# Attention in pairs: both branches of a head in one round of TensorE, values as two half-column products

## The chip, the cores and the metric

The kernel runs on one core of a Trainium2 chip. The metric is device time in microseconds of one execution. TensorE multiplies, ScalarE (ACT) and VectorE (DVE) move results out of PSUM and do the element-wise work, GpSimd (POOL) and SyncE (SP) start transfers. A profile of one execution gives start and duration of each instruction.

## The reference, cut to what matters

Two layers, each a token mixer and a mixture of experts, on 512 tokens of width 1024. The mixer has two attention branches with 8 heads each: A, sliding-window attention over at most two blocks of 128 keys with a bias and a sink, and B, latent attention over all blocks up to the present one. For both, per head:

```python
# A: s = q k^T * scale - slope * |distance|, sink joins the softmax
p = jnp.exp(s - m); p = p / (jnp.sum(p, axis=-1, keepdims=True) + jnp.exp(sink - m))
o = jnp.einsum('bcgrqk,bckgd->bcqgrd', p.astype(v.dtype), vb)      # head width 64
# B: s = (qn kn^T + qr kr^T) * scale, chunk-causal mask
p = jax.nn.softmax(s, axis=-1)
return jnp.einsum('bhqk,bkhd->bqhd', p.astype(v.dtype), v)         # head width 64
```

The outputs of both branches are projected, gated with sigmoid(h @ w_gate + b_gate) and added to x; then come routing and experts.

## The kernel before, in words

Each engine has one instruction stream, written out by hand; semaphores in a table S join them. The attention stage of a layer goes over 64 units u (NUN = 64): tile t = u // 16 of 128 queries, head h = (u // 2) % 8, branch b_ = u % 2 (0 is A, 1 is B). nk key blocks belong to a unit: t + 1 for B, at most 2 for A. For a unit the work is:

- TensorE, scores(u), L1822: scores into ps[u % 2], so all A units use ps[0] and all B units ps[1]. A unit waits until the maximum of the A unit before has been taken (negm_done), a B unit until the exponential of the B unit before is done (exp_done). In tile 0 the A product is 64 rows deep (L1835), in later tiles it is two fp32r products (L1839, L1840); B is one fp32 product, two records in the trace (L1844).
- VectorE, L1284 (A, a custom operation that writes sa and the maximum) or L1290 (B): the maximum.
- ScalarE, L847 (A, in place in sa, two buffers) or L853 (B, from ps[1] to pr): exponential and its sum; a second small instruction reads the accumulator and signals exp_done.
- TensorE, L1893: nk transposes of the probabilities into ps[3] (A) or ps[4] (B).
- ScalarE L861 copies ps[3] into ptr_a, VectorE L1300 copies ps[4] into ptr_b, one buffer each. Each waits for the values of the same branch's unit before: pv_done >= w - 1 for unit w.
- TensorE, L1909: values, nk products of 128x128 probabilities with 128x64 values into ps[2] or ps[6], four units side by side in a bank.
- VectorE, finish_pair (L1243, L1248): after four units it normalises them into `on`.

TensorE's loop, L1873: in step u it issues scores(u + 1), one gate chunk (six fp32r passes of 512 columns, L1663 to L1665, for u from 1 to 60), the transposes of u and the values of u - 1. At u % 16 = 3 and 6 of tiles 1 to 3 the finished outputs of the tile before are turned (out_turned, L1865) into banks 7 and 5.

Between these, ScalarE's and VectorE's loops over u carry work that TensorE needs later: on ScalarE the gate eviction (gate_out, L835, u % 4 = 1), the high part of the turned outputs (attn_out, L825, u % 16 = 4 and 7), quarters of a weight unit's high part (split_quarter, L655, u % 8 = 1 to 4) and the high part of queries (u = 10, 12, 21, 22, 37, 38); on VectorE the low part of the turned outputs (attn_low, L1090, u % 16 = 4 and 7, behind attn_out), halves of a weight unit's low part (split_half, L1058, u % 8 = 5 and 6), and the low part of queries (rows_low, L1090, u = 12, 15, 23, 24, 39, 40). VectorE's order in a step is: maximum of u; copy to ptr_b of u - 1 (u even); finish_pair (u % 4 = 2); attn_low; rows_low; split_half. ScalarE's is: exponential of u; copy to ptr_a of u - 1 (u odd); attn_out; gate_out; rows_high; split_quarter. The gate product's first chunk of a bank waits for attn_low of that bank.

Behind attention stand the output projections and the experts. There four experts share the array in column tiles of 32 (L2006, L2038), next to full-array products (L1997, L2018).

Of the kernel before, what the change touches and what calls it, by code (L numbers as in the profile page):

```python
# [23 lines left out]
P = 128  # L24
CHUNK = 64
A_KV, A_DIM = 2, 64
# [9 lines left out]
def hybrid_trunk(nc, x, positions, norm_mix, w_in, sinks, q_norm, w_qb, kv_norm, w_kvb, w_gate, b_gate,  # L36
# [3 lines left out]
    NT, KD = T // P, D // P  # L40
    AH = sinks.shape[1]
    AQ = AH * A_DIM
    QR, KVR = w_qb.shape[1], w_kvb.shape[1]
    HEADS = AH
# [4 lines left out]
    VD = w_kvb.shape[2] // HEADS - NOPE  # L49
# [54 lines left out]
    with ctx:  # L104
# [24 lines left out]
        ident = sb("ident", [P, P])  # L129
# [60 lines left out]
        av = sb("av", [P, NT, A_KV * A_DIM], F32, 42 * KB)  # L190
        v = sb("v", [P, NT, HEADS * VD], F32, 44 * KB)
# [14 lines left out]
        pr = sb("pr", [P, T], F32, 148.25 * KB)  # L206
        ptr_a = sb("ptr_a", [P, 2 * P], F32, 150.25 * KB)
        ptr_b = sb("ptr_b", [P, T], F32, 151.25 * KB)
        sa = sb("sa", [P, 2, 2 * P + 8], F32, 153.25 * KB)
# [80 lines left out]
        ps = [ctx.enter_context(nc.psum_tensor(f"ps{i}", [P, 512], F32)) for i in range(8)]  # L290
# [13 lines left out]
        S = {n: sem(n) for n in d_names}  # L304
# [1353 lines left out]
        def _(pe):  # L1658
            MM = nc.tensor.matmul
# [16 lines left out]
            for l in range(L):  # L1676
# [42 lines left out]
                for k in range(KD):  # L1719
# [9 lines left out]
                    for m in range(AH // 2 + 1):  # L1729
                        if (k, m) == (0, NT):  # L1730
                            pe.wait_ge(S["h1l_done"], NT + 1)
                        last = mm3(ps[m][:, :], *part(n, k, m * P, P), h1h[:, k, :], h1l[:, k, :], k == 0, k == KD - 1)
# [43 lines left out]
                for i in range(NT + 1):  # L1776
                    if i < NT:
                        o, tok = 4 * (i % 2), slice(i * P, (i + 1) * P)
# [5 lines left out]
                        for half in range(2):  # L1784
                            for k in range(KQ):
                                n = n0 if k < 2 else n0 + 1
                                last = mm3(ps[o + half][:, 0:hq], ch[:, k, tok], cl[:, k, tok],
                                           *part(n, k, half * hq, hq), k == 0, k == KQ - 1)
# [6 lines left out]
                        for two in range(2):  # L1795
                            for k in range(KKV):
                                wk = [w.rearrange("p (h two d) -> p two h d", two=2, d=NOPE)[:, two]
                                      for w in part(n0 + 2, k, 0, HEADS * 2 * NOPE)]
                                last = mm3(ps[o + 2 + two][:, :], ch[:, KQ + k, tok], cl[:, KQ + k, tok], *wk,
                                           k == 0, k == KKV - 1)  # L1800
                        last.then_inc(S["qkv_ps" if i < NT - 1 else "unit_used"], 1)
                    if i >= 1:
                        t, o = i - 1, 4 * ((i - 1) % 2)
                        pe.wait_ge(S["q_roped"], t + 1)
                        for h in range(HEADS):
                            last = nc.tensor.transpose(ps[o + h // 4][0:QD, (h % 4) * P:(h % 4 + 1) * P],
                                                       qc[t % 2][:, h, :], ident[:, :])
# [4 lines left out]
                        for h in range(HEADS):  # L1812
                            last = nc.tensor.transpose(ps[o + 2 + h // 4][0:QD, (h % 4) * P:(h % 4 + 1) * P],
                                                       kc[t % 2][:, h, :], ident[:, :])
# [3 lines left out]
                NUN = NT * 2 * HEADS  # L1818
# [3 lines left out]
                def scores(u):  # L1822
                    t, h, b_ = u // (2 * HEADS), (u // 2) % HEADS, u % 2
                    if u >= 2:
                        pe.wait_ge(S["exp_done" if b_ else "negm_done"], u - 1)
                    if u == 1:
                        pe.wait_ge(S["pool_in"], 32)
                    dst, tok = ps[u % 2], slice(t * P, (t + 1) * P)
                    if b_ == 0:
                        k0 = max(t - 1, 0) * P  # L1830
                        g = h // (AH // A_KV)
                        rows = slice(g * A_DIM, (g + 1) * A_DIM)
                        j, cols = h % (AH // A_KV), slice(k0, (t + 1) * P)
                        if t == 0:
                            last = MM(dst[:, 0:P], aq[rows, 0, j, :], ak[rows, cols], start=True, stop=True)  # L1835
                        else:
                            if h == 0:
                                pe.wait_ge(S["al_done"], 2 * A_KV + t * A_KV)
                            MM(dst[:, 0:2 * P], qs[t][:, g, j, :], ks[:, g, cols], start=True, stop=False)  # L1839
                            last = MM(dst[:, 0:2 * P], qs[t][:, g, j, :], kx[:, g, cols], start=False, stop=True)  # L1840
                    else:
                        n = (t + 1) * P
                        rows = slice(0, QD + NT)
                        last = MM(dst[:, 0:n], qt[rows, h, tok], kt[rows, h, 0:n], start=True, stop=True)  # L1844
                    last.then_inc(S["s_ps"], 1)

                def gate_chunk(m, i):
                    n = U_G[0] + m // 2
                    if i == 0:
                        weights_in(n)  # L1850
                        if m == 0:
                            pe.wait_ge(S["qt_ev"], 2 * NT)
                        if m >= 2:
                            pe.wait_ge(S["g_ev"], m - 1)
                        if m >= 4 and m % 4 == 1:
                            pe.wait_ge(S["otl_done"], 2 * (m // 4) - 1)
                        if m >= 4 and m % 4 == 2:
                            pe.wait_ge(S["otl_done"], 2 * (m // 4))
                    for k in (2 * i, 2 * i + 1):
                        a, c = part(n, k, (m % 2) * P, P)  # L1860
                        last = mm3(ps[7 if m % 2 else 5][:, :], a, c, h1h[:, k, :], h1l[:, k, :], k == 0, k == KD - 1)
                    if i == 3:
                        last.then_inc(S["unit_used" if m % 2 else "g_ps"], 1)

                def out_turned(t, br_, bank):  # L1865
                    pe.wait_ge(S["on_done"], 4 * t + 4)
                    for k in range(KO):
                        last = nc.tensor.transpose(ps[bank][:, k * P:(k + 1) * P], on[:, br_, k * P:(k + 1) * P],
                                                   ident[:, :])
                    last.then_inc(S["ot_ps"], 1)  # L1870

                scores(0)
                for u in range(NUN + 1):  # L1873
                    if u >= 2 * HEADS and u < NUN and u % (2 * HEADS) == 6:
                        pe.wait_ge(S["g_ev"], (u - 2) // 4)
                        out_turned(u // (2 * HEADS) - 1, 1, 5)
                    if u + 1 < NUN:
                        scores(u + 1)
                    if 1 <= u <= 4 * (2 * KD - 1):
                        gate_chunk((u - 1) // 4, (u - 1) % 4)  # L1880
                    if u >= 2 * HEADS and u < NUN and u % (2 * HEADS) == 3:
                        pe.wait_ge(S["g_ev"], (u - 3) // 4)
                        out_turned(u // (2 * HEADS) - 1, 0, 7)
                    if u < NUN:
                        t, h, b_ = u // (2 * HEADS), (u // 2) % HEADS, u % 2
                        nk = t + 1 if b_ else min(t + 1, 2)
                        pe.wait_ge(S["exp_done"], u + 1)
                        if u >= 2:
                            pe.wait_ge(S["pt_dve" if b_ else "pt_act"], u // 2)
                        for k in range(nk):  # L1890
                            src = (pr[:, k * P:(k + 1) * P] if b_ else
                                   sa[:, h % 2, (2 - nk + k) * P:(3 - nk + k) * P])
                            last = nc.tensor.transpose(ps[3 + b_][:, k * P:(k + 1) * P], src, ident[:, :])  # L1893
                        last.then_inc(S["pt_ps"], 1)
                    w = u - 1
                    if w >= 0:
                        t, h, b_ = w // (2 * HEADS), (w // 2) % HEADS, w % 2
                        nk = t + 1 if b_ else min(t + 1, 2)
                        pe.wait_ge(S["pt_dve" if b_ else "pt_act"], w // 2 + 1)
                        if w == 0:  # L1900
                            pe.wait_ge(S["kt_ev"], 2 * NT)
                        if w % 4 == 0 and w >= 8:
                            pe.wait_ge(S["on_done"], w // 4 - 1)
                        g = h // (AH // A_KV)
                        o, bank = (2 * b_ + h % 2) * VD, 2 if h // 2 % 2 else 6
                        for k in range(nk):
                            val = (v[:, k, h * VD:(h + 1) * VD] if b_ else
                                   av[:, t + 1 - nk + k, g * A_DIM:(g + 1) * A_DIM])
                            last = MM(ps[bank][:, o:o + VD], (ptr_b if b_ else ptr_a)[:, k * P:(k + 1) * P], val,  # L1909
                                      start=(k == 0), stop=(k == nk - 1))  # L1910
                        last.then_inc(S["pv_done"], 1)
                gate_chunk(2 * KD - 1, 0)
                gate_chunk(2 * KD - 1, 1)
                pe.wait_ge(S["g_ev"], 2 * KD - 1)
# [43 lines left out]
                for n in range(*U_OUT):  # L1958
                    weights_in(n)
                    pe.wait_ge(S["ml_done"], plan[n][1] + plan[n][2])  # L1960
                    for i in range(2 * NT):
                        last = out_part(n, i)
# [19 lines left out]
                for s_ in range(1, NT):  # L1982
                    last = MM(ranks_at[:, s_ * NEX:], ones_r[:, :], hot[:, 0:(NT - s_) * NEX], start=False,
                              stop=(s_ == NT - 1))
# [191 lines left out]
```

## Time and profile before

| | us |
|---|---|
| runs shown (3): median | 1720.79 |
| lowest, highest | 1717.28, 1721.17 |
| profiled execution | 1715.99 |
| its span, first to last instruction | 1714.3 |
| TensorE busy | 1583.9 (92%) |
| VectorE busy | 723.3 (42%) |
| ScalarE busy | 490.6 (29%) |
| mean granted TensorE clock | 0.975 |

The profiled execution is the one that all rows come from; what is not in its span is 1.7 us. In the trace an fp32 product appears as two records, each with a weight load (PEld, LDWEIGHTS) and a pass (PE, MATMUL); an fp32r product and a transpose appear as one. The duration of a pass contains its way through the array, which overlaps that of the next; what a pass costs in a row of passes is seen in the chain of waits, where each piece lasts from the end of the one before to its own end. The attention stage of layer 0 lies from about 114 to 277 us, that of layer 1 from about 963 to 1126.

### The profile page before, as it was taken

What the parts mean: (1) busy time and instruction counts of PE and PEld (TensorE: products, weight loads), DVE (VectorE), ACT (ScalarE), POOL (GpSimd) and SP (SyncE); (2) the same over time, 40 slices, a digit from 0 to 9 for tenths busy, and PEclk for the clock granted to TensorE, in tenths of its full rate; (3) what the DMA queues carried; (4) which work ended last, traced back from release to release, by engine and by line L of the source; (5) the groups of instructions that cost most, each with busy time, mean ns of one, the idle gap of its engine ahead of it and who ended that gap; (6) DMA issues with size and microseconds to landing.
All of it is one profiled execution on the core that took longest, in us unless ns stands there. A gap on an engine that the chain in (4) does not pass through costs nothing.

```text
span 1714.3 us, 28980 instructions
## 1 busy us (share of the span) xinstructions
PE 1583.9 (92%) x12270; PEld 1195.5 (70%) x12270; DVE 723.3 (42%) x1585; ACT 490.6 (29%) x1044; POOL 36.3 (2%) x61
## 2 busy tenths in 40 slices
PE   9999999999988979988899999999999889798896
PEld 7988887787655646645489888877876656565563
DVE  5466553633344322323344655545423443232324
ACT  5555544322010101010244655442411010011012
POOL 1000000020000000000000000000200000000000
PEclk9999999999998989999999999999999989899999
DMA  5211115547999999999932211165479999999996
GB/s 176 97 53 50 54 46 199 210 151 324 421 420 420 420 420 420 420 421 421 350 141 66 72 53 50 50 229 207 198 321 420 420 420 420 419 420 421 420 420 253
DMA packets 95063, 467.75 MB, mean 273 GB/s; under 512 B 16620, under 2 KB 33004, under 8 KB 45776
## 3 DMA queue, kind: packets, MB, share of 16 engines
q1 hardware_dynamic: 92944, 459.68, 66.7%
q0 software_dynamic: 1984, 6.12, 1.2%
q8 instruction: 102, 1.67, 0.4%
q14 instruction: 33, 0.27, 0.0%
HBM read 461.56 MB, written 4.21 MB: 272 GB/s over the span
## 4 chain that ended last, share of the span: by engine, by line
PE 74%; DMA 10%; DVE 9%; issue 3%; SPq 2%; ACT 2%; DVEq 0%; POOL 0%; ACTq 0%; POOLq 0%
PE ps L1997 11%; PE ps L2006 10%; DMA we<-in_w 10%; PE ps L1663 10%; PE ps L1665 9%; PE ps L1664 9%; PE ps L2038 6%; PE ps L2029 3%; PE ps L1909 3%; DVE xl L1086 3%; SPq L510 2%; PE ps L1844 2%; PE ps L2030 2%; PE ps L1893 2%; PE ps L2024 1%
## 5 line engine op out<-in xcount | busy, mean ns | idle before, releaser
L2006 PE MATMUL ps<-we,xt 128*32 128x256 f32 x4064 | 249.1, 397 | 41.8 <-DMA we<-in_w 26.0
L2006 PEld LDWEIGHTS ps<-we,xt 128*32 128x32 f32 x4064 | 142.5, 114 | 149.4 <-issue 52.0
L1997 PEld LDWEIGHTS ps<-osel,h6x 128*128 128x128 f32 x2048 | 231.1, 192 | 13.9 <-issue 12.3
L1997 PE MATMUL ps<-osel,h6x 128*128 128x128 f32 x2048 | 237.2, 277 | 1.0 <-DVE osel L1424 1.0
L1086 DVE TENSOR_TENSOR xl<-xl,ps 128x512 f32<-128x512 f32 x256 | 165.8, 684 | 104.2 <-PE ps L2030 103.5
L2029 PE MATMUL ps<-yh,turned 128*128 128x512 f32 x256 | 128.5, 502 | 52.6 <-DVE xl L1086 47.7
L1663 PE MATMUL ps<-h1h,wh 128*128 128x512 f32 x336 | 149.1, 444 | 0.8 <-DVE h1l L1090 0.8
L2029 PEld LDWEIGHTS ps<-yh,turned 128*128 128x128 f32 x256 | 50.3, 197 | 138.9 <-DVE xl L1086 115.4
L920 ACT ACTIVATE xt<-ps 128x512 f32<-128x512 f32 x32 | 19.1, 597 | 401.9 <-PE ps L1997 401.9
L1665 PE MATMUL ps<-h1h,wl 128*128 128x512 f32 x336 | 132.4, 394 | 0.0
L1664 PE MATMUL ps<-h1l,wh 128*128 128x512 f32 x336 | 132.2, 393 | 0.0
L2038 PE MATMUL ps<-we,ht 128*32 128x512 f32 x1024 | 116.5, 594 | 3.8 <-DMA we<-in_w 1.3
L1442 DVE COPY xt<-ps 128x512 f32<-128x512 f32 x32 | 22.1, 691 | 213.7 <-PE ps L1997 213.7
L1090 DVE TENSOR_TENSOR yl<-ps,yh 128x512 fp32r<-128x512 f32 x64 | 41.4, 686 | 159.4 <-ACT yh L948 159.4
L1058 DVE SCALAR_TENSOR_TENSOR wl<-raw,gmix,wh 128x256 fp32r<-128x256 f32 (+2 forms) x192 | 86.8, 514 | 50.4 <-ACT wh L655 50.2
L2030 PE MATMUL ps<-yl,turned 128*128 128x512 f32 x256 | 106.2, 415 | 0.0
L655 ACT ACTIVATE wh<-raw,gmix 128x256 fp32r<-128x256 f32 (+3 forms) x176 | 86.6, 552 | 26.9 <-PE ps L1665 26.9
L2038 PEld LDWEIGHTS ps<-we,ht 128*32 128x32 f32 x1024 | 35.7, 109 | 63.5 <-issue 61.3
L1663 PEld LDWEIGHTS ps<-h1h,wh 128*128 128x128 f32 x336 | 63.7, 189 | 17.4 <-issue 3.4
L1664 PEld LDWEIGHTS ps<-h1l,wh 128*128 128x128 f32 x336 | 63.8, 190 | 14.7 <-issue 3.4
L1665 PEld LDWEIGHTS ps<-h1h,wl 128*128 128x128 f32 x336 | 63.4, 189 | 14.1
L948 ACT ACTIVATE yh<-ps 128x512 fp32r<-128x512 f32 x64 | 35.0, 596 | 109.5 <-PE ps L2038 109.5
(294 smaller groups left out, 2386.9 us busy)
## 6 DMA issues: line engine op xcount, KB each, us to landing
we<-in_w SPq DMA_DIRECT2D x382, 1024.0 KB
raw<-in_w_gate SPq DMA_DIRECT2D x16, 1024.0 KB
raw<-in_w_out SPq DMA_DIRECT2D x8, 1024.0 KB
raw<-in_w_in SPq DMA_DIRECT2D x8, 800.0 KB
raw<-in_w_oa SPq DMA_DIRECT2D x4, 1024.0 KB
raw<-in_w_ob SPq DMA_DIRECT2D x4, 1024.0 KB
raw<-in_w_in SPq DMA_DIRECT2D x4, 960.0 KB
xl<-in_x SPq DMA_DIRECT2D x4, 512.0 KB, 5.1
```

The costliest lines, as they stand in the source:

```text
L655: return nc.scalar.activation(dst, src, ACT.Copy, scale=k)
L1058: return V.scalar_tensor_tensor(dst, src, k, hi.bitcast(F32), ALU.mult, ALU.subtract)
L1086: V.tensor_tensor(xl[:, t, cols], xl[:, t, cols], combine_bank(q, t, h)[:, :], ALU.add).then_inc(S["acc_done"], 1)
L1663: MM(dst, lh, rh, start=first, stop=False)
L1664: MM(dst, lh, rl, start=False, stop=False)
L1665: return MM(dst, ll, rh, start=False, stop=last)
L1909: last = MM(ps[bank][:, o:o + VD], (ptr_b if b_ else ptr_a)[:, k * P:(k + 1) * P], val, start=(k == 0), stop=(k == nk - 1))
L1997: last = MM(ps[c][:, k % 4 * P:(k % 4 + 1) * P], h6x[:, t, k * P:(k + 1) * P], osel[:, t, :, :].rearrange("p i r -> p (i r)"), start=(t == ...
L2006: last = MM(ps[2 + c][i * CAP:(i + 1) * CAP, 0:FE], rows[:, k, i * CAP:(i + 1) * CAP], weights(i)[:, k * FE:(k + 1) * FE], start=(k == 0), ...
L2029: MM(bank[:, :], rows, yh[:, cols], start=True, stop=False)
L2030: return MM(bank[:, :], rows, yl[:, cols], start=False, stop=True)
L2038: last = MM(ps[4 + c][i * CAP:(i + 1) * CAP, :], ht[:, j, i * CAP:(i + 1) * CAP], weights(i)[:, j * D + c * 512:j * D + (c + 1) * 512], st ...
```

## The change: what it does

TensorE's loop goes over 32 pairs p (the two branches of a head) instead of 64 units; the other engines' code and all waits' values stay as they are. A round issues: A scores of the next pair, two gate chunks, B scores of the next pair, transposes of A and of B of this pair, values of A and of B of the pair before. (Outputs of a finished tile are turned at the same u % 16 = 3 and 6.) Each value product is issued twice, for 64 of the 128 probability columns each; the second half writes partitions 64 to 127 of the bank, so each half uses half of the array's columns.

```diff
+                H2 = P // 2
+                def probabilities_turned(u):
...
+                def values(w):
+                    t, h, b_ = w // (2 * HEADS), (w // 2) % HEADS, w % 2
+                    nk = t + 1 if b_ else min(t + 1, 2)
+                    pe.wait_ge(S["pt_dve" if b_ else "pt_act"], w // 2 + 1)
...
+                    for k in range(nk):
...
+                        for i in range(2):
+                            rows = slice(k * P + i * H2, k * P + (i + 1) * H2)
+                            last = MM(ps[bank][i * H2:(i + 1) * H2, o:o + VD], (ptr_b if b_ else ptr_a)[:, rows], val,
+                                      start=(k == 0), stop=(k == nk - 1))
+                    last.then_inc(S["pv_done"], 1)
                 scores(0)
-                for u in range(NUN + 1):
-                    if u >= 2 * HEADS and u < NUN and u % (2 * HEADS) == 6:
...
-                    if u + 1 < NUN:
-                        scores(u + 1)
-                    if 1 <= u <= 4 * (2 * KD - 1):
-                        gate_chunk((u - 1) // 4, (u - 1) % 4)
...
-                            last = MM(ps[bank][:, o:o + VD], (ptr_b if b_ else ptr_a)[:, k * P:(k + 1) * P], val,
-                                      start=(k == 0), stop=(k == nk - 1))
-                        last.then_inc(S["pv_done"], 1)
+                scores(1)
+                for p in range(NUN // 2 + 1):
+                    for u in (2 * p, 2 * p + 1):
+                        if u >= 2 * HEADS and u < NUN and u % (2 * HEADS) == 6:
+                            pe.wait_ge(S["g_ev"], (u - 2) // 4)
+                            out_turned(u // (2 * HEADS) - 1, 1, 5)
+                        if u + 2 < NUN and u % 2 == 0:
+                            scores(u + 2)
+                        if 1 <= u <= 4 * (2 * KD - 1):
+                            gate_chunk((u - 1) // 4, (u - 1) % 4)
+                        if u >= 2 * HEADS and u < NUN and u % (2 * HEADS) == 3:
+                            pe.wait_ge(S["g_ev"], (u - 3) // 4)
+                            out_turned(u // (2 * HEADS) - 1, 0, 7)
+                        if u + 2 < NUN and u % 2 == 1:
+                            scores(u + 2)
+                    if p < NUN // 2:
+                        probabilities_turned(2 * p)
+                        probabilities_turned(2 * p + 1)
+                    if p >= 1:
+                        values(2 * p - 2)
+                        values(2 * p - 1)
```

## Rows read from the trace of the kernel before

**Rows 1.** Page: busy time by engine, share of the span, instructions.
```profile
PE 1583.9 (92%) x12270; PEld 1195.5 (70%) x12270; DVE 723.3 (42%) x1585; ACT 490.6 (29%) x1044; POOL 36.3 (2%) x61
```
**Rows 2.** Stretches: length, busy us of PE, PEld, DVE, ACT, POOL; clock; DMA share; GB/s.
```profile
231.00:271.00 40.00, 40.00 (x239) 32.71 (x237) 19.94 (x51) 20.18 (x51) 0.00 (x0) 1.00 0.16 54
271.00:277.00 6.00, 4.11 (x30) 3.31 (x30) 3.84 (x9) 1.65 (x5) 0.00 (x0) 1.00 0.00 0
277.00:281.00 4.00, 4.00 (x14) 3.34 (x14) 0.42 (x1) 0.00 (x0) 2.93 (x4) 0.57 0.33 59
```
**Rows 3.** Chain of waits, a pair in tile 3: start us, us, what.
```profile
255.28 0.91 PE ps L1844 x2
...
257.79 0.84 PE ps L1909 x8
258.63 0.17 PE ps L1839
258.81 0.12 PE ps L1840
258.93 0.23 PE ps L1663
...
260.75 0.39 PE ps L1909 x4
```
**Rows 4.** Chain of waits among the experts: full array and column tiles of 32.
```profile
403.97 2.59 PE ps L2006 x48
406.56 0.59 PE ps L2018 x4
407.14 3.59 PE ps L2006 x64
...
419.19 0.44 PE ps L2018 x4
```
**Rows 5.** Chain of waits in tile 0: values, row-tiled score product, gate pass.
```profile
141.15 0.17 PE ps L1909 x2
141.32 0.41 PE ps L1835 x2
141.73 0.43 PE ps L1663
```
**Rows 6.** Timeline of DVE in tile 3: start, us, line, operation, out<-in, [idle before].
```profile
248.66 0.69 DVE L1300 COPY ptr_b<-ps 128x512 f32<-128x512 f32 x1 [1.32 <-PE ps L1893]
...
249.95 0.42 DVE L1248 TENSOR_TENSOR on<-ps,rden 128x256 f32<-128x256 f32 x1 [0.51 <-PE ps L1868]
250.29 1.66 DVE L1058 SCALAR_TENSOR_TENSOR wl<-raw,gmix,wh 128x256 fp32r<-128x256 f32 x4
251.87 0.68 DVE L1290 TENSOR_REDUCE negm<-ps 128x1 f32<-128x512 f32 x1
...
254.82 0.47 DVE L1284 CUSTOM_DVE_ANT_0 sa<-ps,dist,nsink 128x256 f32<-128x256 f32 x1
```
**Rows 7.** Timeline of ACT in tile 3.
```profile
234.08 0.68 ACT L835 ACTIVATE gb<-ps,bg 128x512 f32<-128x512 f32 x1
234.65 0.91 ACT L655 ACTIVATE wh<-raw,gmix 128x256 fp32r<-128x256 f32 x2
235.45 0.51 ACT L847 ACTIVATE sa<-sa,negm 128x257 f32<-128x257 f32 x1
...
252.59 0.69 ACT L853 ACTIVATE pr<-ps,negm 128x512 f32<-128x512 f32 x1 [4.61 <-DVE negm L1290]
...
253.27 0.37 ACT L861 ACTIVATE ptr_a<-ps 128x256 f32<-128x256 f32 x1
253.53 0.59 ACT L825 ACTIVATE oth<-ps 128x512 fp32r<-128x512 f32 x1
```
**Rows 8.** Timeline of DVE at the end of tile 0, low part of queries.
```profile
146.14 0.69 DVE L1090 TENSOR_TENSOR qs<-aq,qs 64x512 fp32r<-64x512 f32 x1
```
**Rows 9.** Groups by line, 114 to 277 us: count, busy us, mean ns, idle before it.
```profile
L1839 PE MATMUL ps<-ks,qs 128*128 128x256 f32 x24 | 8.7, 364 | 1.4 <-DVE qs L1090 1.4
```

More of the change, by code:

```diff
@@ L1870, in out_turned @@
                     last.then_inc(S["ot_ps"], 1)
-                scores(0)
-                for u in range(NUN + 1):
-                    if u >= 2 * HEADS and u < NUN and u % (2 * HEADS) == 6:
-                        pe.wait_ge(S["g_ev"], (u - 2) // 4)
-                        out_turned(u // (2 * HEADS) - 1, 1, 5)
-                    if u + 1 < NUN:
-                        scores(u + 1)
-                    if 1 <= u <= 4 * (2 * KD - 1):
-                        gate_chunk((u - 1) // 4, (u - 1) % 4)
[L1881 to L1908, printed above, removed]
-                            last = MM(ps[bank][:, o:o + VD], (ptr_b if b_ else ptr_a)[:, k * P:(k + 1) * P], val,
-                                      start=(k == 0), stop=(k == nk - 1))
-                        last.then_inc(S["pv_done"], 1)
@@ new lines, in _ @@
+                H2 = P // 2
+                def probabilities_turned(u):
+                    t, h, b_ = u // (2 * HEADS), (u // 2) % HEADS, u % 2
+                    nk = t + 1 if b_ else min(t + 1, 2)
+                    pe.wait_ge(S["exp_done"], u + 1)
+                    if u >= 2:
+                        pe.wait_ge(S["pt_dve" if b_ else "pt_act"], u // 2)
+                    for k in range(nk):
+                        src = (pr[:, k * P:(k + 1) * P] if b_ else
+                               sa[:, h % 2, (2 - nk + k) * P:(3 - nk + k) * P])
+                        last = nc.tensor.transpose(ps[3 + b_][:, k * P:(k + 1) * P], src, ident[:, :])
+                    last.then_inc(S["pt_ps"], 1)
@@ new lines, in values @@
+                def values(w):
+                    t, h, b_ = w // (2 * HEADS), (w // 2) % HEADS, w % 2
+                    nk = t + 1 if b_ else min(t + 1, 2)
+                    pe.wait_ge(S["pt_dve" if b_ else "pt_act"], w // 2 + 1)
+                    if w == 0:
+                        pe.wait_ge(S["kt_ev"], 2 * NT)
+                    if w % 4 == 0 and w >= 8:
+                        pe.wait_ge(S["on_done"], w // 4 - 1)
+                    g = h // (AH // A_KV)
+                    o, bank = (2 * b_ + h % 2) * VD, 2 if h // 2 % 2 else 6
+                    for k in range(nk):
+                        val = (v[:, k, h * VD:(h + 1) * VD] if b_ else
+                               av[:, t + 1 - nk + k, g * A_DIM:(g + 1) * A_DIM])
+                        for i in range(2):
[3 more added lines that the diff above has]
+                    last.then_inc(S["pv_done"], 1)
```

## The prediction

> **What bounds the kernel now.** I read the busy shares first: TensorE is busy 92% of the span [rows 1], so time is won or lost on its queue. Then the stretches of the stage that the diff touches. In tile 3 TensorE is busy 40.00 of 40.00 us at the full clock; only at the stage's end, from 271 to 277, is it busy 4.11 of 6 us, and in the stretch behind that its granted clock is 0.57 [rows 2]. So attention is bound by TensorE with almost no idle time, and whatever makes its queue wait is new time. The reader is to see that there is nothing left to hide it in. Then the chain of waits through one head of tile 3 (both branches, 32 such pairs in a layer, 64 in all): it runs from a score product at 255.28 to the end of the A values at 260.75 + 0.39 = 261.14, 5.86 us, all on TensorE. Of that the values take 0.84 us (8 records, branch B) and 0.39 (4 records, branch A) [rows 3]. A record is a weight load with its pass; each fp32 product of 128x128 probabilities with 128x64 values makes two, 0.11 us each although only 64 columns stream. A gate pass of 512 columns takes 0.23, and there are twelve in a pair.
>
> **The change on the array.** Call a product of one key block a block; a pair has 2, 4, 5, 6 blocks in tiles 0 to 3. Now a block costs 2 x 0.11 = 0.22 us. After, it has four records of 64 columns' load and 64 streamed. The nearest rows are the expert products, four column tiles of 32: 48 records of 256 columns take 2.59 us, 54 ns each, where one such pass streams 4 x 54 = 216 ns [rows 4], so the four tiles run beside each other and loads are hidden. Two half tiles should then do two records in the time of one half load, half of 0.11 us, 56 ns: 0.112 us for a block. That is the low end. The high end is that records of two tiles follow each other at the 54 ns of those rows (no shorter spacing is sustained anywhere in them): four are 0.216, nothing gained. I take the low end, since those rows show loads and passes of different tiles overlapping; the high end is rival C.
>
> What a change of tiling costs: four transposes behind the expert products take 0.59 us, behind ordinary ones 0.44, so leaving costs 0.15. The first 64 records behind transposes take 3.59 against 64 x 0.054 = 3.46, so entering costs 0.14 [rows 4]. Row tiling in tile 0 agrees: the two records of the score product take 0.41 and the gate pass behind it 0.43 in place of 0.23 [rows 5]. The change puts both branches' values together, so a pair enters once and leaves once: 0.29. In tile 0 it leaves straight into row tiling, so only 0.15 is new. Moving the B scores behind gate passes rather than behind a 64-column product hides their load, about 0.05 gained. Per pair:
> - tile 0: 2 x 0.112 + 0.15 - 0.05 - 0.34 (two times 0.17, rows 5) = -0.02
> - tile 1: 4 x 0.112 + 0.24 - 0.78 = -0.09
> - tile 2: 5 x 0.112 + 0.24 - 1.01 = -0.21
> - tile 3: 6 x 0.112 + 0.24 - 1.23 [rows 3] = -0.32
> (The 0.78 and 1.01 are made from 0.39 for four records and 0.62 for six, which lies between the rows of four and eight.) Eight heads, two layers: 16 x -0.64 = -10 us. This is all that the change can gain.
>
> **The change on the queues.** ScalarE's and VectorE's code stays as it is, one instruction stream each. Their copies of turned probabilities into ptr_a and ptr_b wait until the values of the pair before are done, for there is one buffer each. Before, these values stood in TensorE's queue ahead of the transposes whose result is copied, so the wait was over when the result came. Now a round turns both branches' probabilities first and ends with both branches' values of the pair before; ptr_b can be filled only after the round's end, though its probabilities were turned long ago. Behind the waiting ptr_b copy stand on VectorE: sometimes the normalising of two heads, sometimes half of a weight split, then the maximum for branch B of the next pair, whose scores are ready. ScalarE's B exponential needs that, and TensorE's next B scores (same bank) and transposes need the exponential. From the values' end TensorE has only this to do first: A scores 0.17 + 0.12, twelve gate passes 2.76, leaving the tiling 0.15, sum 3.2 us [rows 3]. That is the cover. The chain against it in tile 3 [rows 6, 7]: copy 0.61 (0.69 less the 0.08 in which the next one overlaps), maximum 0.7, exponential 0.6, accumulator read 0.2, three hand-overs 0.1: 2.2 us. It fits. But by head of a tile (h = 0 to 7; tiles 1 to 3 where not said):
> - h 3 and h 7: normalising 0.7 and half a split 1.58 in between: 4.5 in tile 3, 4.1 in tile 2, 3.8 in tile 1 (shorter copies), 3.4 in tile 0. For h 7 the wait is 0, 0.6, 0.9 us in tiles 0 to 2. For h 3 TensorE turns outputs first (0.44 more cover), but waits for ScalarE's gate eviction, which now starts behind the A values: about 1.0.
> - h 2: ScalarE's eviction of turned outputs (0.6, behind ptr_a copy, quarter split 0.8 and exponential) and VectorE's low part 0.6 (like that of queries, 0.69, rows 8, less the overlap) stand before the maximum: 0.85.
> - h 4: the same eviction and low part of the second half stand before the A maximum, for which the very first product of TensorE's round waits, so there is no cover at all: ptr_a copy 0.3, eviction 0.6, low part 0.6, the custom op with its read 0.5, and hand-overs: 1.8. In tiles 1 and 2 a low part of queries (0.69, rows 8) comes on top: 2.5. Mean 2.3.
> - h 5: ScalarE's gate eviction 0.6, two quarter splits 1.6, two exponentials: 3.4 against 3.2, 0.2; 0.4 in tile 0, where queries are copied too.
> - first A scores of tile 1: they stand at the round's head, and need the queries' low part [rows 8], which comes behind copy 0.2, normalising 0.7, split 1.6, maximum 0.3, itself 0.7: 3.5 us of waiting, where the kernel before idles 1.4 [rows 9]: 2.1 more.
> - the stage's end: the last exponential comes 4.0 us behind a round's end with 0.2 of transposes to do (3.8), the last copy waits for values again (0.8), and the round before has half the gate passes (0.5): 5.1, of which it loses about 2.3 already (1.9 idle [rows 2], the rest in slow records): 2.8 more.
>
> Sum for a layer: 3 x (0.85 + 1.0 + 2.3 + 0.2) + 1.5 (h 7) + 0.4 + 2.1 + 2.8 = 19.9; two layers 40 us. No DMA and no instruction of another engine is moved; the expert weights are released by gate units at the stage's end, so they shift with it. The next stage starts later by the whole sum.
>
> Net: 40 - 10 = +30 us. Against the profiled run's own 1716 us that is 1746; the median of the runs shown is 1720.8, 4.8 higher, so 1751.
>
> **Rivals.** A, forecast: the waits come as summed. Speaking for it: they follow from order in queues and from durations in rows; most sure is h 4 (13.8 us in all), which has no cover.
> B, other side and gain: the chains fit under the cover. It decides at 3.2 us from values' end to exponential, and at zero for h 4; if ScalarE and VectorE were always ahead, only the array's -10 stays: 1711. Against it: VectorE cannot be ahead of a copy that waits for the values.
> C, the halves do not run beside each other, so a block stays near 0.216: 17 blocks x 16 x 0.104 = +28 on A: 1779. Against it, the 54 ns of four tiles [rows 4]; for it, no row shows half-width loads, nor spacing under 54 ns kept up.
> By the Trainium skill (TensorE: Matmul & The Clock Gate, "Wait — 56ns, not 53.3ns?") the sequencer may spend about 62 ns per matmul when hardware decoding is off. By that rule a block would be 4 x 62 = 248 ns and the time some 9 us above C, about 1788. Here the expert rows keep up 54 ns, so this trace does not agree with that figure; it could still hold something between 28 and 54. The rule has a chance of 0.02, inside C's.
> D, the new idle stretches lower TensorE's clock. In the kernel before, the idle end of the stage is followed by a stretch at 0.57 of full clock [rows 2], which did in 4 us the work of 2.3, 1.7 lost. If each of some four longer waits in a layer did that: +14 on A, 1765.
> That the change does not do what it says (half loads one behind the other in one tiling) leaves a block at 0.22 and needs no switches: the waits' 40 less 64 x 0.05, 1758, within A's own range.
>
> **How the numbers follow.** A 0.67, C 0.13, D 0.05, B 0.10, and 0.05 that half the waits cancel the gain within 0.3% (about what a measurement here tells from no change). The forecast's own range is 1734 to 1766, waits a third off either way. For 8 in 10 it must reach C: 1724 to 1783, leaving out B and the far end. Faster 0.10, same 0.05, slower 0.85.
>
> **What would show it.** In the profile after: the transposes' group and the score products of both branches carry idle time with releaser ScalarE's pr and VectorE's negm, some 20 us a layer; the A scores of the sixth head of tiles 1 to 3 start 1.8 to 2.6 us late; ptr_b copies start with the values' end as releaser; value records come two in 56 ns (C: 54 ns each). DVE and ACT busy times stay. Wrong it would be if TensorE stayed near 40 of 40 us busy in tile 3 (B), or if the stage grew with no idle time (C).

## The result, and the profile after

The changed kernel takes 1768.33 us (median of 5, 1767.44 to 1769.14) against 1720.75 for the kernel before (1716.10 to 1721.17): ratio 1.0285, 95% interval 1.0273 to 1.0297. It is 47.6 us slower; the forecast was 30 slower, in a range that reaches to 62. The profiled execution takes 1768.14 us (span 1766.4). That is 52.1 more in span than the profiled one before, which lay 4.8 below its median, and all of the difference lies in the two attention stages: from the first scores to the last values layer 0 takes 189.7 us, before 163.7; layer 1 189.7, before 163.4. Beside each batch of the experiments below the kernel before ran again: 1720.07, 1719.79 and 1721.22 us; the ratios in brackets are to that run.

First the stretch of layer 0's attention in both kernels, with the columns of [rows 2]; before:

```profile
114.00:278.00 164.00, 160.09 (x923) 132.94 (x922) 90.83 (x268) 89.45 (x252) 0.00 (x0) 1.00 0.16 49
```

and after, with three short stretches behind waits, one late stretch and the whole stage:

```profile
145.00:152.50 7.50, 4.99 (x13) 4.05 (x14) 2.98 (x9) 0.46 (x2) 0.00 (x0) 0.54 0.00 0
179.50:183.20 3.70, 3.70 (x11) 2.88 (x10) 1.41 (x5) 0.67 (x4) 0.00 (x0) 0.54 0.08 16
227.60:230.80 3.20, 3.20 (x9) 2.62 (x10) 2.09 (x6) 1.22 (x4) 0.00 (x0) 0.50 0.00 0
243.00:290.00 47.00, 41.94 (x341) 31.25 (x341) 21.21 (x63) 18.84 (x51) 0.00 (x0) 1.00 0.14 46
114.00:303.00 189.00, 164.27 (x1184) 125.60 (x1185) 87.70 (x267) 86.96 (x252) 0.00 (x0) 0.95 0.13 42
```

TensorE was idle for 3.9 of 164 us and is now idle for 24.7 of 189, 20.8 more. VectorE and ScalarE do 87.70 and 86.96 us of work, no more than the 90.83 and 89.45 before: they have no more to do, they hand over later. And the mean granted clock of the stage is 0.95 where it was 1.00, with stretches at 0.50, the lower of TensorE's two levels (1.2 of 2.4 GHz).

Where the idle time lies is told by the groups by line, 114 to 303 us (busy us, mean ns, then idle time ahead of the group and what ended it):

```profile
L1663 PE MATMUL ps<-h1h,wh 128*128 128x512 f32 x120 | 50.1, 418 | 2.9 <-DVE otl L1090 2.9
L1844 PE MATMUL ps<-kt,qt 100*128 100x128 f32 (+3 forms) x64 | 23.9, 455 | 4.2 <-ACT pr L853 4.0
L1883 PE MATMUL ps<-ident,pr 128*128 128x128 f32 x80 | 14.4, 280 | 2.4 <-ACT pr L853 2.4
L1839 PE MATMUL ps<-ks,qs 128*128 128x256 f32 x24 | 9.6, 399 | 11.2 <-DVE negm L1284 7.3 <-DVE qs L1090 3.9
L1868 PE MATMUL ps<-ident,on 128*128 128x128 f32 x24 | 3.8, 280 | 2.3 <-ACT gb L835 1.4 <-ACT ga L835 0.9
```

The largest is the one with no cover, the A scores (L1839): 7.3 us wait for VectorE's A maximum, 3.9 for the queries' low part, where [rows 9] had 1.4. Gate passes wait for otl (the low part of turned outputs), B scores and transposes for pr (ScalarE's B exponential), the turning of outputs for ScalarE's gate eviction. The other 1.7 us are transposes that wait for sa (1.1) and smaller waits.

One round without a wait, the one from tile 2 to tile 3 (transposes of tile 3's first head, values of tile 2's last), as pieces of the chain (start, us, what):

```profile
254.60 0.86 PE ps L1844 x2
255.46 0.66 PE ps L1883 x6
256.12 0.73 PE ps L1902 x20
256.85 0.32 PE ps L1839
257.17 0.12 PE ps L1840
257.29 0.23 PE ps L1663
```

These answer to [rows 3]. The values of both branches (L1902, here 5 blocks, 20 records) take 0.73 us together, entering included; the A product behind them takes 0.32 in place of 0.17, which is leaving. The array does what the change wants of it.

### The profile page after: what moved, and what is told of

Read it like the earlier page. It is cut to its first block, busy times and chain, and to the rows that moved or that the text cites. A ratio compares the mean times of both kernels' runs of the same rounds, so it can differ in the third digit from the quotient of the medians.

```text
span 1766.4 us, 30068 instructions
## 1 busy us (share of the span) xinstructions
PE 1592.5 (90%) x12814; PEld 1180.4 (67%) x12814; DVE 717.9 (41%) x1585; ACT 486.2 (28%) x1044; POOL 36.3 (2%) x61
## 4 chain that ended last, share of the span: by engine, by line
PE 66%; DVE 11%; DMA 11%; ACT 5%; issue 4%; SPq 2%; DVEq 0%; ACTq 0%
DMA we<-in_w 11%; PE ps L2013 10%; PE ps L2022 10%; PE ps L1663 8%; PE ps L1664 8%; PE ps L1665 8%; PE ps L2054 5%; PE ps L2045 3%; DVE xl L1086 3%; PE ps L1844 2%; PE ps L1902 2%; SPq L510 2%; PE ps L2046 2%; PE ps L1883 2%; DVE wl L1058 2%
## 5 line engine op out<-in xcount | busy, mean ns | idle before, releaser
L2045 PE MATMUL ps<-yh,turned 128*128 128x512 f32 x256 | 127.8, 499 | 52.7 <-DVE xl L1086 47.6
L1663 PE MATMUL ps<-h1h,wh 128*128 128x512 f32 x336 | 138.4, 412 | 6.9 <-DVE otl L1090 5.8
L1300 DVE COPY ptr_b<-ps 128x128 f32<-128x128 f32 (+3 forms) x64 | 31.4, 491 | 151.6 <-PE ps L1902 150.1
```

What stands on the lines that cost most here:

```text
L1663: MM(dst, lh, rh, start=first, stop=False)
L2045: MM(bank[:, :], rows, yh[:, cols], start=True, stop=False)
```

## The experiments

The theory: helper work (maxima, copies, splits, evictions) stands in an order that fits rounds of one unit; pair order makes TensorE wait for it, waits lower the clock, and the halves themselves gain. The rival is that the halves, by switching the tiling, cost the time; for the clock the rival is that it costs nothing beside the waits.

**Pair order alone.** The new order of rounds, each value product whole:

```diff
-                        for i in range(2):
-                            rows = slice(k * P + i * H2, k * P + (i + 1) * H2)
-                            last = MM(ps[bank][i * H2:(i + 1) * H2, o:o + VD], (ptr_b if b_ else ptr_a)[:, rows], val,
-                                      start=(k == 0), stop=(k == nk - 1))
+                        last = MM(ps[bank][:, o:o + VD], (ptr_b if b_ else ptr_a)[:, k * P:(k + 1) * P], val,
+                                  start=(k == 0), stop=(k == nk - 1))
```

> Pair order alone, each value product whole. If the waits made by the pair order are the cause, it is no faster than the changed kernel: about 1775 us (1768 plus some 9 us that the halves gave, less 1 to 3 because the longer B values let ScalarE start earlier), with 18 to 21 us of TensorE idle time in each attention stage. If the half-column products (switches of tiling) are the cause, it falls back to about 1721.

Measured: 1776.19 us (1.0323, 1.0305 to 1.0341), idle time of 21.6 us in layer 0's stage. The pair order alone costs 56 us, so the halves are not the cause; with them the same order took 7.9 less.

**Halves alone.** The old order of units, each value product as two halves (the same two lines as above, put into the kernel before).

> Half-column products alone, in the old order of units, so the tiling is entered and left twice for a pair. If the waits are the cause: about 1726 us (1724 to 1729), by 0.29 us for each of two visits against 0.11 us saved for each block: +0.2, +0.14, +0.03, -0.08 us for a pair in tiles 0 to 3, sixteen pairs each, and idle time as before, 3 to 4 us a stage. If the halves are the cause it is over 1745.

Measured: 1727.30 us (1.0047, 1.0030 to 1.0064), with as little idle time as before:

```profile
114.00:282.00 168.00, 164.29 (x1186) 122.95 (x1186) 90.84 (x266) 89.41 (x252) 0.00 (x0) 1.00 0.15 47
```

Idle 3.7 us, clock 1.00, 4 us more busy. In this order the tiling is entered and left for each unit, and the chain shows why it does not pay (L1911 is the value product):

```profile
250.89 0.62 PE ps L1911 x16
251.51 0.32 PE ps L1839
...
253.75 0.38 PE ps L1911 x8
254.14 0.59 PE ps L1868 x4
```

These pieces lie in tile 3, where B has four blocks and A two. Sixteen half records, entering included, take 0.62 where eight whole ones took 0.84 [rows 3], but eight take 0.38 where four took 0.39; and each time the next product pays 0.15 for leaving. So handling both branches together is what makes the halves pay, and is what makes the waits.

**VectorE's B maximum first.** In the changed kernel, the ptr_b copy and the normalising stand one step later in VectorE's stream, behind the B maximum:

```diff
-                for u in range(NUN + 1):
+                for u in range(NUN + 2):
...
-                    w = u - 1
+                    w = u - 2
...
-                    if u >= 6 and u % 4 == 2:
-                        finish_pair((u - 6) // 4)
+                    if u >= 7 and u % 4 == 3:
+                        finish_pair((u - 7) // 4)
```

> The changed kernel with VectorE taking the B maximum ahead of the waiting ptr_b copy and of the normalising, one step earlier than now. If the maximum behind the waiting copy causes the waits of heads 3 and 7, of the first A scores of tile 1 (partly) and of the stage's end: some 8 us less in each stage, about 1750 us (1744 to 1755); the waits of head 4 (2.8, 2.7, 1.8 us), which stand behind ScalarE's ptr_a copy, stay. If these waits have another cause: 1768.

Measured: 1752.16 us (1.0185, 1.0168 to 1.0202). The groups for B scores, B transposes and A scores:

```profile
L1844 PE MATMUL ps<-kt,qt 100*128 100x128 f32 (+3 forms) x64 | 23.4, 447 | 1.4 <-ACT pr L853 1.3
L1883 PE MATMUL ps<-ident,pr 128*128 128x128 f32 x80 | 14.0, 273 | 0.2 <-ACT pr L853 0.2
L1839 PE MATMUL ps<-ks,qs 128*128 128x256 f32 x24 | 9.4, 390 | 11.2 <-DVE negm L1284 7.3 <-DVE qs L1090 3.9
```

The waits for pr go from 4.2 + 2.4 to 1.4 + 0.2 us a stage, those of the A scores stay to the tenth, and the time fell by 16.2 us, 8.1 a stage, as expected. That part of the expectation that counted on tile 1's first A scores was wrong: their 3.9 us are unchanged, because the copy and the normalising, moved one step later, still stand ahead of the queries' low part.

**Waiting busy.** The changed kernel with passes in front of the longest waits; they write columns of bank 2 that nothing reads:

```diff
+                BUSY = {14: 28, 24: 20, 40: 20, 56: 12}
+                def busy_passes(n):
+                    for _ in range(n):
+                        MM(ps[2][:, 256:512], upper_r[:, :], upper_r[:, :].rearrange("p (o q) -> p o q", o=1)
+                           .to_broadcast([P, 2, P]), start=True, stop=True)
...
+                        if u in BUSY:
+                            busy_passes(BUSY[u])
                         if u + 2 < NUN and u % 2 == 0:
                             scores(u + 2)
```

> The changed kernel with passes whose result nobody reads (28, 20, 20, 12 of 256 columns, 0.11 us each) in front of the four longest waits of a stage, so that TensorE waits busy: 3.1, 2.2, 2.2, 1.3 us inside waits of 3.9, 2.8, 2.7, 1.8. If the lower clock behind the waits costs time of its own: full clock there, and 9 to 12 us less, 1756 to 1759. If only the waits count: unchanged, 1768.

Measured: 1759.33 us (1.0229, 1.0211 to 1.0246), 9.0 us less than the changed kernel. The timeline of TensorE at the wait of head 5's A scores in tile 1, then the stretches that answer to the first and last of the changed kernel:

```profile
174.04 2.65 PE L1910 MATMUL ps<-upper_r 128*128 128x256 f32 x20
176.94 0.39 PE L1839 MATMUL ps<-ks,qs 128*128 128x256 f32 x1 [0.25 <-DVE negm L1284]
```

```profile
145.00:152.50 7.50, 7.09 (x50) 6.06 (x49) 3.61 (x12) 1.01 (x5) 0.00 (x0) 1.00 0.00 0
114.00:298.00 184.00, 169.63 (x1272) 131.78 (x1272) 87.82 (x267) 87.22 (x252) 0.00 (x0) 0.99 0.14 44
```

The scores still wait for the same maximum, yet layer 0's stage is 5.4 us shorter and layer 1's 6.0, with the clock at 0.99 for 0.95; the rest of that profiled execution took 2.4 us longer, and no run shows why. The lower clock costs time of its own.

**The wait without cover, alone.** In the changed kernel VectorE's low part of the second half of turned outputs moves from ahead of head 4's A maximum to behind it (queries' pieces of tiles 2 and 3 with it):

```diff
-                    if u >= 2 * HEADS and u % (2 * HEADS) == 7:
+                    if u >= 2 * HEADS and u < NUN and u % (2 * HEADS) == 8:
                         attn_low(u // (2 * HEADS) - 1, 1, 5)
...
-                    if u in (12, 15, 23, 24, 39, 40):
-                        rows_low(u // (2 * HEADS) + 1, 0 if u in (12, 23, 39) else 1)
+                    if u in (12, 15, 24, 25, 40, 41):
+                        rows_low(u // (2 * HEADS) + 1, 0 if u in (12, 24, 40) else 1)
```

> The changed kernel with one helper moved: VectorE's low part of the second half of turned outputs (and of queries) stands behind head 4's A maximum instead of ahead of it. If that order makes the wait of head 5's A scores, which has no cover: the waits of 2.8, 2.7 and 1.8 us go, with their refill and the lower clock behind two of them some 10 us a stage, 1748 us (1744 to 1753). If these scores wait for the copies or the array: 1768.

Measured: 1751.21 us (1.0174, 1.0157 to 1.0191), 17.1 less than the changed kernel. What the order did is seen in the changed kernel's chain in tile 3:

```profile
276.68 0.41 PE ps L1902 x8
...
277.17 0.38 ACT ptr_a L861
277.55 0.50 ACT oth L825
...
278.07 0.04 DVE otl L1090
278.11 0.57 issue
278.68 0.14 DVE sa L1282
278.83 0.39 DVE sa L1284
...
279.28 0.39 PE ps L1839
```

Copy to ptr_a, eviction, low part (0.04 + 0.57), maximum, then the scores; TensorE has nothing in between but the B values that end at 277.53. With the low part moved, the same line reads

```profile
L1839 PE MATMUL ps<-ks,qs 128*128 128x256 f32 x24 | 9.4, 390 | 3.9 <-DVE qs L1090 3.9
```

All 7.3 us are gone, and with them the low stretches behind two of these waits: 8.6 us a stage in all, where 10 were expected.

**All helpers' order fitted.** On VectorE this has the third experiment's order and new places for the low parts. On ScalarE the evictions stand ahead of the waiting ptr_a copy; their six old lines behind the copy, where the first test was `== 4`, go. Only the new lines are shown:

```diff
+                    if u >= 2 * HEADS and u % (2 * HEADS) == 3:
+                        attn_out(u // (2 * HEADS) - 1, 0, 7)
+                    if u >= 2 * HEADS and u % (2 * HEADS) == 7:
+                        attn_out(u // (2 * HEADS) - 1, 1, 5)
+                    if u >= 5 and u % 4 == 1:
+                        gate_out((u - 5) // 4)
                     w = u - 1
                     if w >= 0 and w % 2 == 0:
...
+                    if u >= 2 * HEADS and u < NUN and u % (2 * HEADS) == 5:
+                        attn_low(u // (2 * HEADS) - 1, 0, 7)
+                    if u >= 2 * HEADS and u < NUN and u % (2 * HEADS) == 8:
+                        attn_low(u // (2 * HEADS) - 1, 1, 5)
...
+                    if u in (12, 14, 24, 25, 40, 41):
+                        rows_low(u // (2 * HEADS) + 1, 0 if u in (12, 24, 40) else 1)
```

> The changed kernel with the helpers' order fitted to the pairs: on VectorE the B maximum first as in the third experiment, the low parts of turned outputs and of queries at places with cover; on ScalarE turned outputs and gate eviction ahead of the waiting ptr_a copy. If the loss of 48 us was waits and the clock behind them, nearly all of it goes and the gain of the halves, 5 to 6 us a stage, is left: 1712 us (1707 to 1720), some 5 us of idle time a stage. If pair order costs something of its own: 1730 or more.

Measured: 1705.85 us, ratio to the kernel before 0.9924 (0.9910 to 0.9938): 62 us less than the changed kernel, 0.8% under the kernel before, and below the 1707 to 1720 expected.

```profile
114.00:272.00 158.00, 154.64 (x1193) 121.66 (x1192) 89.06 (x267) 87.20 (x252) 0.00 (x0) 1.00 0.16 51
```

Idle 3.4 us, clock 1.00, and TensorE busy 154.6 where it was 160.1.

**The same with whole products:**

> The kernel of the run before with whole value products. Less the waits, only the halves differ: 9 to 12 us slower than it, about 1722 us (1717 to 1730), near the kernel before. If the halves gained nothing once the waits are gone: the same as the run before.

Measured: 1713.27 us (0.9968, 0.9956 to 0.9980). The halves are worth 7.4 us where 9 to 12 were expected, and the time lies below the expected 1717 to 1730: this kernel too is 6.5 us faster than the one before. The profile shows part of that, 1.7 and 1.5 us in the two stages, mostly less idle time; the rest was not isolated. A pair of tile 3 with halves, then whole (L1900):

```profile
245.01 0.85 PE ps L1902 x24
```

```profile
246.88 1.29 PE ps L1900 x12
```

**Queries one step earlier.** In the fitted kernel tile 1's first A scores still waited 1.4 us; `(12, 14, 24, ...)` becomes `(12, 13, 24, ...)`.

> The kernel with all helpers' order fitted, and the second low part of queries for tile 1 one step earlier still, ahead of the weight split (1.67 us) that stands before it there. If that split is what tile 1's first A scores still wait for: their 1.4 us of idle time goes in each stage, 1702 us (1700 to 1705). If they wait for something behind it: 1706 as before.

Measured: 1703.78 us (0.9895, 0.9879 to 0.9912), 2.1 less than the fitted kernel. The group's idle time falls from 1.4 to 0.6 us, not to nothing, and its releaser is now the maximum:

```profile
L1839 PE MATMUL ps<-ks,qs 128*128 128x256 f32 x24 | 9.2, 383 | 0.6 <-DVE negm L1284 0.6
```

In layer 1 of the fitted kernel the same 1.4 us wait had been followed by a stretch at the lower clock:

```profile
987.00:990.20 3.20, 3.20 (x10) 2.53 (x9) 2.63 (x11) 0.46 (x2) 0.00 (x0) 0.50 0.00 0
```

In its layer 0 the same wait was followed by none, and with the wait of 0.6 neither layer has one. This is the fastest kernel here, 1% under the kernel before.

## Why the prediction was right, and where it was short

**The gain on the array: right in size.** Entering 0.14 and leaving 0.15 were taken from the experts' rows [rows 4]; the rows after show leaving as 0.32 for 0.17. A block was to cost 0.112 us. Between 5 and 6 blocks of a pair the values grow from 0.73 (rows above) to 0.85, so 0.12 a block. Rival C is out: it wanted 54 ns for a record, and a record takes 29 to 30. The sum was -10 us for the whole, 5.1 a stage. From first scores to last values of layer 0 the kernel before, the fitted one with whole products and the fitted one with halves give:

```profile
114.10:277.80 163.70, 159.78 (x922) 132.72 (x922) 90.71 (x267) 89.35 (x252) 0.00 (x0) 1.00 0.16 49
113.80:275.80 162.00, 159.48 (x923) 133.58 (x922) 89.16 (x267) 87.00 (x252) 0.00 (x0) 1.00 0.15 50
114.00:272.10 158.10, 154.74 (x1194) 121.73 (x1193) 89.06 (x267) 87.20 (x252) 0.00 (x0) 1.00 0.16 51
```

Busy time falls by 5.0 us, so the size is right, but its parts are not as priced. The halves alone give 4.7, where the terms without the 0.05 for moved B scores had said 3.5; the pair order alone gives 0.3, where those 0.05 came to 1.6. One reason is in the rows: the values of a pair, whole and together, take 1.29 us, not the 0.84 + 0.39 of the sum. In the whole time the halves gave 7.4 rather than 9.4 us: the kernel with halves idles 0.8 us more in this stage and has the stretch at the lower clock in layer 1.

**The waits: right.** The sum said 19.9 us a stage, the profile has 20.8 more idle time. By term, in layer 0: A scores of the fifth round of tiles 1 to 3 (h 4) 2.5, 2.5, 1.8 foreseen, 2.8, 2.7, 1.8 measured; first scores of tile 1 3.5 foreseen, 3.9 measured (before 1.4); h 7 of tiles 1 and 2 0.6 and 0.9 foreseen, 0.5 and 0.8 measured; the stage's end 5.1 foreseen, 4.4 measured. The turning of outputs was to wait for ScalarE's gate eviction, and does (2.3 of the 3.0 foreseen for h 3; the B scores behind it wait 1.5 more). One wait has its size but another waiter: at h 2 the 0.85 each were foreseen for what needs the B maximum, and it is the gate pass that waits for the low part directly, 2.9 in all. So of "some 20 us" foreseen with releasers pr and negm the rows show 6.4 and 7.3. The orders behind the waits are shown by three experiments: moving the B maximum took out most of the waits for pr and no others; moving the low parts took out the 7.3 and no others; moving all of them took out nearly everything. The waits for otl and for the gate eviction went only in that last run, so their cause was not tested alone.

**What was short: the price of a wait, 17 us in all** (1768.33 against 1751; 22 between the profiled executions). The prediction priced a wait at its idle time, and put the lower clock among the rivals (D, 0.05, +14 us) as if it could come only instead of A. It comes with A: the idle stretches of 3.9, 2.8 and 2.7 us and those of the stage's end are followed by stretches at half of the full clock, and passes of 512 columns take 0.43 us there for 0.23, as in this chain behind the 3.9 us wait:

```profile
144.87 1.58 DVE wl L1058 x4
...
146.68 0.70 DVE qs L1090
...
147.51 0.55 PE ps L1839
...
148.28 0.43 PE ps L1663
```

The second missing term is the restart, which the prediction put at nothing: the first pass behind a wait takes longer at the full clock too. The B scores of tile 3 take 1.13 us behind a wait of 0.84 and 0.86 without one; a gate pass takes 0.47 behind a wait of 0.84 and 0.23 otherwise:

```profile
249.01 1.13 PE ps L1844 x2
...
254.60 0.86 PE ps L1844 x2
...
265.66 0.47 PE ps L1663
266.13 0.23 PE ps L1664
```

I read this as a first pass whose way through the array nothing overlaps. The A scores and the turning of outputs lose only 0.07 at the full clock, since they have the leaving of the tiling to pay in any case.

The changed kernel and the fitted one can be laid side by side, for TensorE's order is the same in both: the same 1192 passes from first scores to last values of layer 0, 189.7 us and 158.1. Summed from each pass's end to the next one's, the 31.6 between them are 21.4 of idle time, 6.4 more in passes at the lower clock and 3.8 more in first passes at the full one. The busy waits, which gave 5.4 us back in this stage and left the low stretch at its end, agree with these 6.4. Against the kernel before a stage then adds up as 20.8 idle + 6.4 clock + 3.8 restart - 5.0 array = 26.0, which is what was measured.

**The rivals.** B was out, as the h 4 wait with no cover had said. C is out. D should have been a term. The forecast's own range, to 1766, missed the time by 2 us, and would have been 1738 to 1764 by its "a third off". The range that held it had been stretched to 1783 for C, which was the wrong reason; that was luck. With the lower clock and the restart as terms the forecast would have been about 1771, 20 above 1751, against 1768.

## What to carry to other kernels

When the order of one engine's stream is changed, write down for every single-buffered copy on the other engines what it waits for now and what stands behind it there; the helpers' order is part of the change, and here it turned 48 us of loss into 17 of gain. Price a wait on TensorE at its idle time, plus the restart (0.07 to 0.27 us here), plus the lower clock that can follow: here behind all waits of 2.7 us and more, and once behind 1.4, but not behind one of 2.4. Narrow tiles pay only if the work in them is gathered, since each visit costs 0.29 us: 24 half records in one visit took 0.44 us less than the whole ones, with 0.15 to pay for leaving; eight took no less.

## What the runs showed of the hardware

- Two tiles of half the array's columns ran their fp32 records, load included, at 29 to 30 ns each (0.73 to 0.85 us for four more). A record of the whole array took 0.11 us with twice the columns to load, and the quarter tiles with 256 columns streamed took 54 ns. A single half tile was not run, so how much comes from the shorter load and how much from overlap is not shown.
- Behind waits of 3.9, 2.8 and 2.7 us the granted clock was 0.50, the lower level (the stretches of 7.5 and 3.7 us above hold some full clock and read 0.54); from 243 to 290 us, with a wait of 1.8 and shorter ones, it stayed 1.00. With the longest waits filled by passes it stayed 1.00 there. A wait of 1.4 us in the fitted kernel was followed by a low stretch in layer 1 and by none in layer 0, and one of 2.4 us, in the run of the pair order alone, by none: the length of the wait alone does not decide.
- Behind a wait the first pass took longer at the full clock: 0.27 us more for B scores, 0.24 for a gate pass.
